# Memory projections of a two-layer decoder block spread over the gaps ahead of the first attention, and a PSUM bank of its own for one partial sum of the down projection

## The reference

```
memn = layer_norm(mem, ln_mem_g, ln_mem_b)
for l in range(2):
    h = x @ w_in[l]                       # latents, queries, keys, values, compressed k and v, gates
    o_a = mla_mixer(...)                  # latent attention, 8 heads of 96 columns
    o_b = nsa_mixer(...)                  # compressed, selected and window keys, gated
    x = layer_norm(ALPHA * x + concat(o_a, o_b) @ w_out[l])
    k, v = split(memn @ xa_wkv[l])        # 4 heads of 256: keys 1024 columns, values 1024
    x = layer_norm(ALPHA * x + attend(x @ xa_wq[l], k, v) @ xa_wo[l])
    x = layer_norm(ALPHA * x + conv_ffn(x))          # up 5632 columns, down 2816 rows
```

## Time and profile before

| | us |
|---|---|
| median of 3 runs | 1887.33 |
| lowest and highest | 1879.38, 1890.71 |
| the profiled execution, its time | 1886.46 |
| its span from first to last instruction | 1884.7 |

### The profile page before, as it was taken

How to read it: one execution, slowest core, us unless ns; L and a number is a source line. 1 busy time by engine, 2 the same in 40 slices (tenths; PEclk the granted TensorE clock), 3 DMA queues, 4 the chain that set the end, 5 groups by cost and what they waited for, 6 DMA issues and landing times.

```text
span 1884.7 us, 22064 instructions
## 1 busy us (share of the span) xinstructions
PE 1788.7 (95%) x8510; PEld 1320.7 (70%) x8510; DVE 1049.9 (56%) x2080; ACT 362.6 (19%) x885; POOL 190.9 (10%) x126
## 2 busy tenths in 40 slices
PE   7999999988899999998999999999989999999997
PEld 5886488643746886476866759984658766689953
DVE  5766555443754776642640058995714620369985
ACT  1111000141501111103520212220023501222210
POOL 1212111000020222120001000002110000000020
PEclk9999999989999999998799999999996999999999
DMA  9644364512064554436016425543453044254440
GB/s 317 198 141 172 120 216 151 179 67 89 24 209 158 178 179 156 154 111 206 1 45 211 134 95 166 164 179 130 139 153 117 1 156 147 77 196 157 163 156 23
DMA packets 162502, 265.59 MB, mean 141 GB/s; under 512 B 4008, under 2 KB 105684, under 8 KB 162270
## 3 DMA queue, kind: packets, MB, share of 16 engines
q1 hardware_dynamic: 157470, 248.18, 39.4%
q0 software_dynamic: 4768, 15.48, 2.4%
q10 hardware_dynamic: 160, 0.52, 0.1%
HBM read 262.56 MB, written 1.08 MB: 140 GB/s over the span
## 4 chain that ended last, share of the span: by engine, by line
PE 73%; DVE 15%; DVEq 4%; ACT 4%; issue 2%; DMA 1%; SPq 1%; ACTq 0%
PE psum L757 14%; PE psum L917 11%; PE psum L813 9%; PE psum L720 8%; PE psum L730 7%; PE psum L707 6%; PE psum L1035 3%; PE psum L1070 3%; DVE work L2229 3%; PE psum L968 2%; PE psum L1052 2%; DVE ring L1745 2%; PE psum L956 2%; PE psum L869 2%; PE psum L855 2%
## 5 line engine op out<-in xcount | busy, mean ns | idle before, releaser
L601 POOL TENSOR_TENSOR work<-ring,work 128x1024 f32<-128x1024 f32 (+1 forms) x57 | 141.5, 2483 | 812.0 <-DVE work L1747 812.0
L917 PE MATMUL psum<-ring,work 128*128 128x512 f32 x352 | 161.6, 594 | 0.0
L1743 DVE TENSOR_TENSOR work<-ring 128x1024 f32<-128x1024 f32 (+1 forms) x83 | 99.1, 1194 | 89.8 <-PE psum L917 87.3
L730 PE MATMUL psum<-ring,x_t 128*128 128x512 f32 x320 | 140.0, 595 | 7.4 <-ACT x_t L1307 7.4
L1887 DVE CUSTOM_DVE_ANT_0 work<-psum,work 128x256 f32<-128x256 f32 (+1 forms) x96 | 31.4, 364 | 192.7 <-PE psum L1035 192.6
L917 PE MATMUL psum<-work 128*128 128x512 f32 x264 | 125.4, 604 | 6.2 <-DVE work L2262 6.1
L917 PEld LDWEIGHTS psum<-ring,work 128*128 128x128 f32 x352 | 67.1, 192 | 82.4 <-issue 82.3
L730 PEld LDWEIGHTS psum<-ring,x_t 128*128 128x128 f32 x320 | 60.0, 190 | 81.5 <-issue 71.8
L1745 DVE TENSOR_TENSOR ring<-ring 128x1024 f32<-128x1024 f32 (+1 forms) x83 | 102.3, 1233 | 6.9 <-issue 0.9
L1747 DVE TENSOR_TENSOR work<-ring 128x1024 f32<-128x1024 f32 (+1 forms) x83 | 99.6, 1200 | 6.2
L917 PEld LDWEIGHTS psum<-work 128*128 128x128 f32 x264 | 50.2, 193 | 69.8 <-issue 60.0
(11 more groups left out here) (251 smaller groups left out, 2950.8 us busy)
## 6 DMA issues: line engine op xcount, KB each, us to landing
ring<-in_ffn_w_up_dram SPq DMA_DIRECT2D x66, 1024.0 KB, 7.9
ring<-in_w_in_dram SPq DMA_DIRECT2D x21, 2048.0 KB, 8.0
ring<-in_ffn_w_down_dram SPq DMA_DIRECT2D x20, 2048.0 KB, 7.8
ring<-in_ffn_w_gate_dram SPq DMA_DIRECT2D x22, 1024.0 KB, 5.5
ring<-in_xa_wkv_dram SPq DMA_DIRECT2D x8, 2048.0 KB, 8.1
ring<-in_w_out_dram SPq DMA_DIRECT2D x6, 2048.0 KB, 8.8
ring<-in_xa_wq_dram SPq DMA_DIRECT2D x4, 2048.0 KB, 8.5
ring<-in_xa_wo_dram SPq DMA_DIRECT2D x4, 2048.0 KB, 7.7
```

Source lines behind the costliest of these rows:

```text
L601: nc.gpsimd.tensor_tensor(t4, quarters(n, chunks, pitch)[2], t2, ALU.subtract).then_inc(fourth_ready, 1)
L730: return mm(bank(banks[2 * i + h]), acts[:, c, i * P:(i + 1) * P], ring[:, (n0 + c // 4) % RING, o:o + 512], start=(c == 0), stop=(c == KD ...
L917: last = mm(sums[p], acts[p][:, q, :], rhs[:, i, :], start=(q == 0), stop=(q == KF // 2 - 1))
```

## The change

The two key panels of `xa_wkv` are projected between the compressed keys and the latent turns, in halves, the first value panel whole ahead of the first attention; the second value panel stays behind the output product. TensorE's new order from the key turns on is: first half of the first key panel; compressed keys; second half; compressed values; four latent turns; first half of the second key panel; four latent turns; second matmul of the compression; second half of the key panel; a wait until ScalarE has copied both key panels out; first value panel into banks 1 and 3; first attention (whose scores use only banks 0 and 2 of the first four); output product, now in banks 2 to 5; second value panel into banks 0 and 1. The loads follow the same order. ScalarE copies the first key panel behind `rows_ready` 18, the second behind the compressed keys, and the first value panel inside the attention (`between`, before it takes the third unit out of PSUM). The compressed products go to banks 6 and 7, `H_CMP` and VectorE's signal for it disappear. Memory keys, values and queries get other places in SBUF, over columns of the first projection that are used up by then. In the down projection of the two layers product 7 goes to bank 4, which nothing uses there, and products 3 and 4 to banks 0 and 1; the wait for the last up panel moves from product 7 to product 3.

```
-V_XQT, V_XKT, V_XV = 0, 2048, 4096
+V_XQT, V_XK, V_XV = 5488, (0, 1976), ((1024, 3000), (3952, 4464))
...
-LAYER_PANELS = [1] * 4 + [1] * 2 + [2] * 2 + [1] * 2 + [1] * 4 + [1] * 2 + [1] * 2 + [2] * UPS + [1] * DOWNS
+LAYER_PANELS = [1] * 4 + [1] * 2 + [2, 1, 2, 1] + [1] + [1] * 2 + [1] + [1] * 2 + [1] * 2 + [2] * UPS + [1] * DOWNS
...
+L_CMP, L_WK, L_WV = ([N_FIRST + x for x in pair] for pair in ((6, 8), (7, 9), (10, 13)))
...
+        def totals(l):
+
+            order = (5, 6, 7, 3, 0, 1, 2) if l is None else (5, 6, 7, 3, 4, 0, 1)
+            return {p: bank(b) for p, b in zip(STREAM, order)}
...
-                        if d == 0 and p == 7:
+                        if d == 0 and p == (3 if l is not None else 7):
                             pe.wait_ge(group_free, g_last + 1)
...
+                def memory_keys(j, blocks):
+
+
+                    n = at(L_WK[j], N_LAYER, l)
+                    if 0 in blocks:
+                        arrived(n)
+                    o = group(H_WK + j, l)
+                    for c in blocks:
+                        for k in range(KD):
+                            last = mm(o[:, c * T:(c + 1) * T], ring[:, n % RING, k * 512 + c * P:k * 512 + (c + 1) * P],
+                                      MEMT[:, k, :], start=(k == 0), stop=(k == KD - 1))
+                    if 3 in blocks:
+                        last.then_inc(panel_done, 1)
...
+                memory_keys(0, (0, 1))
+                pe.wait_ge(comp_in, at(1, 1, l))
+                compressed(0)
+                memory_keys(0, (2, 3))
+                compressed(1)
+                pe.wait_ge(rows_ready, at(18, PER_Y, l))
+                for j in range(4):
+                    turn_latent_heads(j)
+                memory_keys(1, (0, 1))
+                for j in range(4, 8):
+                    turn_latent_heads(j)
                 pe.wait_ge(comp_hid, at(1, 1, l))
...
+                memory_keys(1, (2, 3))
...
+                pe.wait_ge(group_free, at(H_WK + 2, G_LAYER, l))
+                memory_values(0, (0, 1), (1, 3))
                 pe.wait_ge(turned_out, at(E_MLA + 8, B_LAYER, l))
                 pe.wait_ge(comp_used, at(1, 1, l))
                 pe.wait_ge(pads_zero, 5 + l)
                 attend(UNITS_2, U1, l)
-                residual_product(L_OUT, XT, (0, 1, 4, 5), turn_mixed(E_O, U1 + TT + 12, 19, l), l)
-
-                weight_stationary(L_WK, H_WK, MEMT, l)
-                pe.wait_ge(half_ready, at(11, PER_NORM, l))
-                weight_stationary(L_WK + 1, H_WK + 1, MEMT, l)
-                for j in range(2):
-                    rows_stationary(L_WV + j, [H_WV + j], MEMT, KD, 512, 512, l)
+                pe.wait_ge(group_free, at(H_WV + 2, G_LAYER, l))
+                residual_product(L_OUT, XT, (2, 3, 4, 5), turn_mixed(E_O, U1 + TT + 12, 19, l), l)
+
+                memory_values(1, (0, 1), (0, 1))
...
+                attend(UNITS_2, U1, l, {4: lambda: memory_values(0, (1, 3), 2)})
```

More of the change, by code:

```diff
@@ L328, in two_blocks_kernel @@
         CWT = w(V_CWT, 4, 44)
-        XQT, XKT, XV = w(V_XQT, KD, T), w(V_XKT, KD, T), w(V_XV, TT, D)
+        XQT, XK = w(V_XQT, KD, T), [w(o, 4, T) for o in V_XK]
+        XV = [[w(o, 512) for o in halves] for halves in V_XV]
         mem_in = w(W_MEM, TT, D)
@@ L1074, in attend @@
                 for j in range(n + 3):
+                    if j in between:
+                        between[j]()
                     if j < n:
@@ L1260, in _, with memory_values @@
                 last.then_inc(comp_out, 1)
+                memory_keys(1, (2, 3))
+                def memory_values(j, tiles, banks):
+                    n = at(L_WV[j], N_LAYER, l)
+                    if 0 in tiles:
+                        arrived(n)
+                    for i in tiles:
+                        for k in range(KD):
+                            last = mm(bank(banks[i]), MEMT[:, k, i * P:(i + 1) * P], ring[:, n % RING, k * 512:k * 512 + 512],
+                                      start=(k == 0), stop=(k == KD - 1))
+                    if 1 in tiles:
+                        last.then_inc(panel_done, 1)
+                pe.wait_ge(group_free, at(H_WK + 2, G_LAYER, l))
+                memory_values(0, (0, 1), (1, 3))
                 pe.wait_ge(turned_out, at(E_MLA + 8, B_LAYER, l))
@@ L1369, in first_copies, with attend @@
                 hidden(UPS - 1)
-            def attend(units, u0, l=None):
+            def attend(units, u0, l=None, between={}):
                 def exps(j):
@@ L1536, in _, with projected, turned_latent_heads @@
                     turned_columns(b)
+                def projected(n, g, scale, dst):
+                    act.wait_ge(panel_done, at(n + 1, N_LAYER, l))
+                    activation(dst, psum_pair(g).rearrange("p (a b) -> p a b", a=4), ACT.Copy, scale=scale).then_inc(group_free, 1)
+                def turned_latent_heads(j):
+                    dst = QTM if j < 4 else KTM
+                    batch_out(E_MLA + j, dst[0:MQ, 2 * (j % 4):2 * (j % 4) + 2, :], MQ, l)
+                act.wait_ge(rows_ready, at(18, PER_Y, l))
+                projected(L_WK[0], H_WK, 1.0, XK[0])
+                for j in range(4):
+                    turned_latent_heads(j)
                 act.wait_ge(sig_in, at(2, PER_SIG, l))
@@ L1540, in _ @@
                 activation(ngate, ngate, ACT.Exp, scale=-1.0).then_inc(sig_exp, 1)
-                for j in range(8):
-                    dst = QTM if j < 4 else KTM
-                    batch_out(E_MLA + j, dst[0:MQ, 2 * (j % 4):2 * (j % 4) + 2, :], MQ, l)
+                for j in range(4, 8):
+                    turned_latent_heads(j)
                 act.wait_ge(comp_out, at(1, 1, l))
@@ L1546, in _, with memory_values @@
                 copy(vc, PO[0:NC, 512:640].rearrange("p (g n) -> p g n", g=2)).then_inc(comp_used, 1)
-                attend(UNITS_2, U1, l)
+                projected(L_WK[1], H_WK + 1, 1.0, XK[1])
+                def memory_values(j, banks, groups):
+                    act.wait_ge(panel_done, at(L_WV[j] + 1, N_LAYER, l))
+                    for i in range(TT):
+                        last = copy(XV[j][i], bank(banks[i]))
+                    last.then_inc(group_free, groups)
+                attend(UNITS_2, U1, l, {4: lambda: memory_values(0, (1, 3), 2)})
                 turned_rows(E_O, XT, l)
-                def projected(n, g, scale, dst):
-                    act.wait_ge(panel_done, at(n + 1, N_LAYER, l))
-                    activation(dst, psum_pair(g).rearrange("p (a b) -> p a b", a=4), ACT.Copy, scale=scale).then_inc(group_free, 1)
                 rstd_tiles(15, l)
[L1554 to L1557, removed]
+                memory_values(1, (0, 1), 1)
                 turned_rows(E_X1, XT, l)
```

48 lines of the change are left out of this document (23 added, 25 removed).

## The result

| | before | after |
|---|---|---|
| median, us | 1887.84 (4 runs, 1879.38 to 1890.71) | 1854.95 (4 runs, 1852.26 to 1856.98) |
| profiled execution, us | 1886.46 | 1856.59 |
| its span, us | 1884.7 | 1854.8 |
| mean granted clock | 0.968 | 0.982 |

The ratio is 0.9833, with a 95% interval of 0.9803 to 0.9863: 1.7% faster. The two spans differ by 29.9 us, the two medians by 32.9. Two single executions of the kernels further down, 2567.02 us (pieces joined) and 3733.13 us (half of the first tile inside too), were far slower than all the others and are left out of their numbers.

What follows compares the result with a forecast made beforehand. TensorE, busy 95% of the span, was taken as the bound, with only gaps and low-clock stretches to win. 10.7 + 12.3 + 2.6 + 7.0 = 32.6 us off 1886.46 gave 1853.9, forecast as 1855 us, range 1848 to 1862 (0.60).

Steps and rivals of the forecast that it cites:

- Compressed keys: Between the key halves: 64 matmul records of 30 columns at 11 a microsecond, 5.8 us.
- Latent turns and waits: Eight latent-turn batches 5.4 us; wait for ScalarE's latent copies 0.3 us; new wait before the value panel 1.1 us.
- new stretch: Key turns to first attention: 13.3 us besides moved work, against 24.0 and 25.6; 10.7 and 12.3 us won.
- First attention: 58.9 us in both layers: 2.6 us won in layer 0, none in layer 1; bounds 53.5 and 61.5 us.
- Cover: Behind the output product, one 13.8 us value panel still covers VectorE's norm, 7.8 us spare; without any, 6 us a layer.
- Loads: Weight panels for the moved work: four slots suffice, lateness put at zero.
- Down projection: At its start the wait falls from 3.05 to 1.35 us and 1.8 us of low clock goes: 3.5 us a layer.
- The sum: Whole kernel: 10.7 + 12.3 + 2.6 + 7.0 = 32.6 us won, forecast 1855 us.
- The clock did not fall in the compressed pieces: Rival that it falls there all the same: up to 3.5 us a piece, four pieces, 1862 to 1869 us; chance 0.19.
- Gaps only: Rival: only waits are won, clock and attention stay as they were: 10.3 us, 1877 us; chance 0.08.
- Attention at full clock: Rival: the first attention keeps the clock too, 5.4 us less in each layer, 1844 us; chance 0.10.
- Slower: Rival: clock stays at 1.2 GHz from the first compressed piece to the attention, some 33 us a layer, 1945 us; chance 0.03.

Runs made afterwards that it cites:

- pieces joined: Kernel after, with the whole first key panel ahead of both compressed panels, which run together as 64 records: 1863.92 us, ratio 0.9869.
- half of the first tile inside too: Kernel after, with half of the first value panel's first tile and its whole second tile in chunks inside the first attention: 1843.07 us, ratio 0.9761.
- gap kernel: Kernel after, with both compressed panels ahead of both key panels again, the rest of the move kept: 1876.07 us, ratio 0.9949.
- the bank alone: Kernel before, with only the down projection's new order of totals and its moved wait: 1877.67 us, ratio 0.9953.

## Why the prediction was right, point by point

- **Compressed keys: mis-sized.** 5.8 us forecast, 7.0 measured (32 records from 876.99 to 880.48, 3.49 us, twice). The error is in the reading of the earlier trace rows: the count in brackets takes every record that lies in the microsecond even in part, so 11 are about 9.2 starts and 7 about 4.7 (64 records in 13.67 us at 0.50, from 1408.98 to 1422.65 in the gap kernel). The kernel after has x11 in such a microsecond too, for 109 ns a record. The 107 ns of the Trainium skill ("TensorE: Matmul & The Clock Gate", "LDWEIGHTS (loading the stationary operand)") agree with it at clock 1.00. The page names no clock; "at either clock" was my reading of it, and the 214 ns a record of the gap kernel at 0.50 speak against that. My doubt of the size was wrong, my claim that the rate follows the clock right.
- **Latent turns and waits: nearly as forecast.** Turns 4.6 us (2.27 and 2.34, with a wait of 0.25 in each group) for 5.4; waits 0.38 for 0.3 and 1.11 for 1.1. The moved work took 42.0 us (a key half 6.9 to 7.2) for 41.4. The new stretch won 9.7 and 11.4 us for 10.7 and 12.3: the 1.0 us missing in layer 0 is 1.2 of the compressed keys, 0.6 of the moved work and 0.1 of the first wait, less 0.8 of the turns and 0.1 of the six small matmuls.
- **First attention: the number as forecast, in part by luck.** 2.5 and -0.2 us for 2.6 and 0. The low time behind the K units stays, as expected. But the 61.5 us of layer 0 were that one execution's: with the bank alone and the same old order it was 58.6 us, and 60.1 in layer 1. The 24.0 us of the stage ahead of it were short to match (26.1 there). So only the sum of the two stages carries the forecast: 23.0 + 2.6 = 25.6 us for both layers, measured 23.4.
- **Cover: held.** Needed 6.0 us of 13.8, as read. Its price without any was 7.5 us for an estimate of 6: the wait cost 4.6, less than that, and the clock behind it 3.0, which the estimate didn't have.
- **Loads: right.** No wait of TensorE for a key or value panel in either layer.
- **Down projection: right.** 3.4 us a layer for 3.5, in the kernel after and with the bank alone. The clock's half of it was read off one gap of 1.4 us that had left the clock up, and it held.
- **The sum.** 32.6 us forecast, 29.9 measured between the two spans: 1.9 us of the new stretch, 0.3 of the attention, 0.1 of the down projection and 0.7 in the first block, which no edit touches, make the difference, to within 0.3. The medians differ by 32.9 us, which agrees with the sum better than its terms do: that 1855 us was met to the tenth is luck.
- **Rivals.** The clock did not fall in the compressed pieces of the profiled execution. It is a real mechanism, though, and this order doesn't exclude it: joined pieces lose it in both layers, and of the 18 layers in the nine profiled executions with the pieces cut as here 7 lose it at the first piece. There the key half behind it takes 8.48 to 8.84 us instead of 7.15, and in three of them the piece itself 3.89 to 4.02 instead of 3.65. The price is 1.7 us each time, and not 3.5, as only the end of the piece is slow, if at all; the second piece never lost the clock. Gaps only: excluded by the clock of 1.00 in the new stretch and by the gap kernel, where two waits of 5.6 us together and the pieces joined behind them cost 21 us. That its 1876 us lies near this rival's 1877 is chance. Attention at full clock: not so in the kernel after, but its bound of 53.5 us was about right: 52.9 us once dense chunks lie between the K units, with 5.1 and 4.6 us of it from the clock for the 5.4 forecast and the rest from covered waits. Slower: nothing of it; in the gap kernel dense matmuls do bring the clock back, after 1.6 and 2.9 us of loss.

## What to carry to other kernels

Work that nothing waits for is worth most in a gap in front of sparse matmuls and between them: first look which stretch has a granted clock below 1.00 and an idle gap ahead of it, and put dense independent work into that gap. Cut it finely: the same first key panel did 21 us more for the program in halves ahead of and between the sparse pieces than behind them, and a further 15 us came from half a panel spread over the next sparse stage (2 of them by a wait that went with it). Pieces of 3.5 us between dense ones are short enough most times, not always. Leave enough of it where it covers another engine, here 6 us of 13.8 behind the product. A missing cover costs more than its wait, as the clock falls behind it as well.

## What had not been expected of the hardware

- A stretch of 9.9 us of 30-column matmuls, with a full TensorE ahead and no idle in it, took the clock to 0.50 (mean 0.70), in both layers. Pieces of 3.49 us between dense halves ran at 1.00 in the kernel after; in 7 of 18 layers of such kernels the first of them still set off a fall that cost 1.7 us.
- Behind the gaps of 2.49 and 3.15 us the 64 records took 12.08 and 13.67 us from start to start, at mean clocks of 0.57 and 0.50: 189 and 214 ns a record, against 109 at full clock. A narrow f32 matmul with its weight load loses half its rate with the clock.
- With dense chunks between the K units the attention is 52.9 us long. So 5 of its 59 us were the clock alone and 1 short waits, though its mean clock was 0.88 and TensorE in it was 97% busy.
- A dense panel of 14 us at full clock doesn't protect what follows: behind it the first K scores took 4.38 to 4.44 us in ten attentions, but 5.93, 5.78, 5.24 and 4.90 us in four others. Why is open.
